# State-space heads: y products of all eight heads of a group in one burst, gating moved to later weight chunks

## The reference, cut to what matters

```
cum    = cumsum(dt * a)                                # per head, over the tokens
decay  = exp(where(causal, cum_i - cum_j, -inf))       # per head: token i, token j
cb     = C_i . B_j                                     # per group
y_i    = sum_j (cb * decay)_ij * (x_j * dt_j)          # per head, 64 columns
y      = (y + d_skip * x) * silu(z)
y      = rms_norm(y over the 512 columns of the group)
x,B,C  = silu(causal_depthwise_conv(u @ W_xBC) + bias) # width 4
```

## Time and profile before

| | |
|---|---|
| runs | 2046.87, 2047.00, 2047.02 us |
| span of the profiled execution, first to last instruction | 2045.1 us |
| own device time of the profiled execution | not listed; the median of the runs lies 1.9 us above its span |
| PE busy | 2033.3 us (99%), 10999 matrix products |
| DVE busy | 1326.1 us (65%) |
| ACT busy | 1044.2 us (51%) |
| POOL busy | 14.5 us (1%) |
| mean granted clock of PE | 0.999 |
| bytes moved by DMA | 388.12 MB, mean 190 GB/s |

### The profile page before, as it was taken

How to read it: one execution, slowest core, us unless ns; L and a number is a source line. 1 busy time by engine, 2 the same in 40 slices (tenths; PEclk the granted TensorE clock), 3 DMA queues, 4 the chain that set the end, 5 groups by cost and what they waited for, 6 DMA issues and landing times.

```text
span 2045.1 us, 31288 instructions
## 1 busy us (share of the span) xinstructions
PE 2033.3 (99%) x10999; PEld 1746.4 (85%) x10999; DVE 1326.1 (65%) x1897; ACT 1044.2 (51%) x1313; POOL 14.5 (1%) x29
## 2 busy tenths in 40 slices
PE   9999999999999999999999999999999999999998
PEld 8888888888888888998888888888888888888886
DVE  7788888888864444676555576665665665444476
ACT  6566666665554444445444465444444444444464
POOL 0000000000000000000000000000000000000000
PEclk9999999999999999999999999999999999999999
DMA  8666666666565565445556656666666666555554
GB/s 236 197 195 192 186 196 192 177 194 195 165 206 189 185 201 185 129 123 175 190 186 227 241 171 197 185 187 194 185 194 188 183 194 226 193 191 193 204 197 144
DMA packets 332351, 388.12 MB, mean 190 GB/s; under 512 B 25896, under 2 KB 248608, under 8 KB 330624
## 3 DMA queue, kind: packets, MB, share of 16 engines
q1 hardware_dynamic: 329184, 369.86, 58.0%
q0 software_dynamic: 2928, 17.21, 2.4%
q10 hardware_dynamic: 176, 0.20, 0.0%
HBM read 384.00 MB, written 3.21 MB: 189 GB/s over the span
## 4 chain that ended last, share of the span: by engine, by line
PE 99%; DMA 0%; DVE 0%; ACT 0%; SPq 0%; issue 0%; DVEq 0%
PE acc L508 16%; PE acc L521 15%; PE acc L727 14%; PE acc L728 14%; PE acc L729 14%; PE acc L526 8%; PE acc L510 8%; PE acc L666 1%; PE acc L898 1%; PE acc L484 1%; PE acc L486 1%; PE acc L485 1%; PE acc L824 1%; DMA raw<-w_in_in 0%; PE acc L589 0%; PE acc L761 0%
## 5 line engine op out<-in xcount | busy, mean ns | idle before, releaser
L1576 DVE TENSOR_TENSOR wlo<-raw,whi 128x1024 fp32r<-128x1024 f32 (+1 forms) x703 | 849.3, 1213 | 558.8 <-ACT whi L1118 556.9
L1118 ACT ACTIVATE whi<-raw 128x1024 fp32r<-128x1024 f32 (+1 forms) x704 | 736.1, 1049 | 680.1 <-PE acc L729 398.8
L508 PE MATMUL acc<-u,whi 128*128 128x512 f32 x1408 | 488.6, 394 | 0.0
L510 PE MATMUL acc<-u,wlo 128*128 128x256 f32 x1408 | 390.2, 277 | 0.0
L727 PE MATMUL acc<-whi,g 128*128 128x512 f32 x848 | 330.2, 389 | 0.0
L729 PE MATMUL acc<-whi,g 128*128 128x512 f32 x848 | 329.9, 389 | 0.0
L728 PE MATMUL acc<-wlo,g 128*128 128x512 f32 x848 | 329.9, 389 | 0.0
L521 PE MATMUL acc<-u,whi 128*128 128x512 f32 x1376 | 328.7, 391 | 0.0
L508 PEld LDWEIGHTS acc<-u,whi 128*128 128x128 f32 x1408 | 264.0, 187 | 61.4 <-issue 0.2
L521 PEld LDWEIGHTS acc<-u,whi 128*128 128x128 f32 x1376 | 252.7, 188 | 48.8
L510 PEld LDWEIGHTS acc<-u,wlo 128*128 128x128 f32 x1408 | 264.3, 188 | 0.0
(11 more groups left out here) (329 smaller groups left out, 1545.9 us busy)
## 6 DMA issues: line engine op xcount, KB each, us to landing
raw<-w_in_in SPq DMA_DIRECT2D x208, 512.0 KB, 4.1
raw<-w_gate_in SPq DMA_DIRECT2D x88, 512.0 KB, 4.5
raw<-w_up_in SPq DMA_DIRECT2D x88, 512.0 KB, 4.5
raw<-w_down_in SPq DMA_DIRECT2D x88, 512.0 KB, 3.6
raw<-w_ssm_o_in SPq DMA_DIRECT2D x64, 512.0 KB, 4.0
raw<-w_in_in SPq DMA_DIRECT2D x64, 256.0 KB, 4.1
raw<-w_attn_o_in SPq DMA_DIRECT2D x32, 512.0 KB, 4.2
raw<-w_out_in SPq DMA_DIRECT2D x32, 512.0 KB, 4.5
```

Source lines behind the costliest of these rows:

```text
L508: T.matmul(bank(b), wh[:, j, i * P:i * P + P], src[:, kt, :, :].rearrange("p a s -> p (a s)"), start=start and j == 0, stop=False, skip_gr ...
L510: last = T.matmul(bank(b)[:, 0:SEQ], wl[:, j, i * P:i * P + P], src[:, kt, 0, :], start=False, stop=stop and j == len(kts) - 1, skip_group ...
L1118: S.activation(whi[:, slot, 0:w], raw[:, slot, 0:w], ACT.Copy).then_inc(sem("hi_ready"), 1)
L1576: V.tensor_tensor(wlo[:, slot, 0:w], raw[:, slot, 0:w], whi[:, slot, 0:w].bitcast(F32), ALU.subtract) \
```

## The change: what it does

- PE: the products behind chunk 4 go away, and all four pairs of heads are multiplied behind chunk 10, in one piece. Pairs 0 and 1 go to the two halves of bank 7, pairs 2 and 3 to those of bank 6 (`y_place`). PE signals `y_mm` after two pairs, not after each.
- `e` has eight slots and a place of its own in SBUF. `decays` waits no longer for PE. Its calls for pairs 2 and 3 move from chunks 8 and 9 to 7 and 8, the Exps from 9 and 10 to 8 and 9, the masks from 9 and 10 to 8 and 9.
- DVE: `y_gate` of pairs 0 and 1 moves from chunks 8 and 9 to chunk 12, that of pairs 2 and 3 from chunks 13 and 14 to chunk 14.
- Convolution of x pair 1, `conv_first` on ACT and `conv_rest` on DVE: from chunk 11 to chunk 13.
- The SBUF area reserved for the descriptors of POOL's DMAs shrinks from 16384 to 2048 bytes of each partition, which makes room for the larger `e`.

```diff
+SCRATCH = 2048
...
-    START = 16512
-    CONST0 = START
+    START = SCRATCH + 128
+    E0 = START
+    CONST0 = E0 + HPG * 384 * 4
...
-    e = at("e", [P, 4, 384], G0 + 32 * 2048)
+    e = at("e", [P, HPG, 384], E0)
...
+    def y_place(p):
+
+        return 7 - p // 2, p % 2 * SEQ
...  PE, ssd_step
-            if c_ in (4, 10):
-                p0 = 0 if c_ == 4 else 2
-                if p0 == 0:
-                    pe.wait_ge(sem("xdt_ready"), it * 2)
-                else:
-                    pe.wait_ge(sem("y_skip"), it * 4 - 2)
-                pe.wait_ge(sem("masked"), it * 8 - 8 + 2 * p0 + 4)
-                for p in (p0, p0 + 1):
-                    b = 7 - p % 2
+            if c_ == 10:
+                pe.wait_ge(sem("xdt_ready"), it * 2)
+                pe.wait_ge(sem("masked"), it * 8)
+                for p in range(4):
+                    b, at_col = y_place(p)
...
-                    last.then_inc(sem("y_mm"), 1)
+                    if p % 2:
+                        last.then_inc(sem("y_mm"), 1)
...  ACT, ssm_main
-            if c_ in (11, 15):
-                i = (c_ - 11) // 4
+            if c_ in (13, 15):
+                i = (c_ - 13) // 2
                 if not head:
                     act.wait_ge(sem("y_skip"), it * 4 + (2 * i - 2))
                 conv_first(it, 1 + i, (2 * i, 2 * i + 1))
...  ACT, ssm_side
-            if c_ in (5, 6, 9, 10):
+            if c_ in (5, 6, 8, 9):
...  DVE, ssm_main
-            if c_ == 11:
+            if c_ == 13:
                 conv_rest(it, 1, (0, 1))
...  DVE, decays
-                if hd >= 4:
-                    dve.wait_ge(sem("y_mm"), it * 4 - 4 + (hd - 4) // 2 + 1)
...  DVE, y_gate
-            dve.wait_ge(sem("y_mm"), it * 4 - 3 + p)
+            dve.wait_ge(sem("y_mm"), it * 2 - 1 + p // 2)
...  DVE, ssm_side
+            if c_ == 7:
+                decays(it, 2)
             if c_ == 8:
+                decays(it, 3)
+                mask_scores(it, 2)
+            if c_ == 9:
+                mask_scores(it, 3)
+            if c_ == 12:
                 y_gate(it, 0)
-                decays(it, 2)
-            if c_ == 9:
-                decays(it, 3)
                 y_gate(it, 1)
-                mask_scores(it, 2)
-            if c_ == 10:
-                mask_scores(it, 3)
-            if c_ == 13:
+            if c_ == 14:
                 y_gate(it, 2)
-            if c_ == 14:
                 y_gate(it, 3)
...
-    nc = bacc.Bacc("TRN2", target_bir_lowering=False, num_devices=1)
+    nc = bacc.Bacc("TRN2", target_bir_lowering=False, num_devices=1, dynamic_dma_scratch_size=SCRATCH)
```

More of the change, by code:

```diff
@@ L652, in ssd_step @@
                 last.then_inc(sem("xtr_mm"), 1)
-            if c_ in (4, 10):
-                p0 = 0 if c_ == 4 else 2
-                if p0 == 0:
-                    pe.wait_ge(sem("xdt_ready"), it * 2)
-                else:
-                    pe.wait_ge(sem("y_skip"), it * 4 - 2)
-                pe.wait_ge(sem("masked"), it * 8 - 8 + 2 * p0 + 4)
-                for p in (p0, p0 + 1):
-                    b = 7 - p % 2
-                    ea, eb = e[:, 2 * p % 4, :], e[:, (2 * p + 1) % 4, :]
+            if c_ == 10:
[3 more added lines that the diff above has]
+                    b, at_col = y_place(p)
                     for blk, o, n in ((0, 0, 256), (1, 256, 128)):
-                        for i, ee_ in enumerate((ea, eb)):
+                        for i in range(2):
                             half = slice(64 * i, 64 * i + 64)
-                            last = T.matmul(bank(b)[half, SEQ - n:SEQ], xdt[:, blk, p, half], ee_[:, o:o + n],
-                                            start=blk == 0, stop=blk == 1, skip_group_check=True,
-                                            tile_position=(0, 64 * i))
-                    last.then_inc(sem("y_mm"), 1)
+                            last = T.matmul(bank(b)[half, at_col + SEQ - n:at_col + SEQ], xdt[:, blk, p, half],
+                                            e[:, 2 * p + i, o:o + n], start=blk == 0, stop=blk == 1,
+                                            skip_group_check=True, tile_position=(0, 64 * i))
+                    if p % 2:
+                        last.then_inc(sem("y_mm"), 1)
             if c_ == 14:
@@ L1229, in ssm_side @@
                 S.preload_act_table_set("natural_log_exp_and_others")
-            if c_ in (5, 6, 9, 10):
-                p = (5, 6, 9, 10).index(c_)
+            if c_ in (5, 6, 8, 9):
+                p = (5, 6, 8, 9).index(c_)
                 for hd in (2 * p, 2 * p + 1):
                     act.wait_ge(sem("seg"), it * 16 - 16 + 2 * hd + 2)
-                    S.activation(e[:, hd % 4, :], e[:, hd % 4, :], ACT.Exp).then_inc(sem("decay"), 1)
+                    S.activation(e[:, hd, :], e[:, hd, :], ACT.Exp).then_inc(sem("decay"), 1)
             if c_ == 14:
@@ L1755, in decays @@
             for hd in (2 * p, 2 * p + 1):
-                if hd >= 4:
-                    dve.wait_ge(sem("y_mm"), it * 4 - 4 + (hd - 4) // 2 + 1)
                 for blk, o, n in ((0, 0, 256), (1, 256, 128)):
-                    V.tensor_scalar(e[:, hd % 4, o:o + n], cumb[:, hd, SEQ - n:SEQ], cum_g[:, blk, hd:hd + 1],
+                    V.tensor_scalar(e[:, hd, o:o + n], cumb[:, hd, SEQ - n:SEQ], cum_g[:, blk, hd:hd + 1],
                                         0.0, ALU.subtract, ALU.min).then_inc(sem("seg"), 1)
@@ L1764, in mask_scores @@
                 dve.wait_ge(sem("decay"), it * 8 - 8 + hd + 1)
-                V.tensor_tensor(e[:, hd % 4, :], e[:, hd % 4, :], cbm[:, :], ALU.mult).then_inc(sem("masked"), 1)
+                V.tensor_tensor(e[:, hd, :], e[:, hd, :], cbm[:, :], ALU.mult).then_inc(sem("masked"), 1)
         def x_dt(it, blk):
@@ L1780, in y_gate @@
             V.scalar_tensor_tensor(yb[:, p % 2, :], xs[:, p, :], gp_side[:, 4 + p:5 + p],
-                                       bank(7 - p % 2)[:, 0:SEQ], ALU.mult, ALU.add).then_inc(sem("y_skip"), 1)
+                                       bank(y_place(p)[0])[:, y_place(p)[1]:y_place(p)[1] + SEQ], ALU.mult, ALU.add).then_inc(sem("y_skip"), 1)
             dve.wait_ge(sem("y_skip"), it * 4 - 3 + p)
```

## The result

Five runs of the changed kernel gave 2058.68 to 2058.95 us, median **2058.8 us**, against 2047.0 us before: ratio 1.0058, 95% interval 1.0047 to 1.0069: slower, by 0.6%. The prediction was 2058.9 us. The profiled execution has a span of 2057.2 us (12.1 more than before).

The account below looks back on a forecast made before the run. PE bounds the kernel, never waiting in the changed stretch. Per loop group 1.81 + 0.10 - 0.19 = +1.72 us, +12.0 over seven, -0.19 in the last: +11.9, giving 2058.9 us; range 2053 to 2065 us.

Parts of the forecast that it names:

- The signs to look for: Seven PE waits of 1.3 us at the squares' product, seven of 0.5 at chunk 16; loop groups of 62.4 us.
- The queue of DVE: DVE's work from the burst's start: squares ready after 15.44 us, split of chunk 16 after 18.98 us.
- B: Start of PE's burst behind chunk 10, from which the forecast counts all later times in a loop group.
- PE's need: After the burst's start PE reaches the squares' product at 14.14 us and would start chunk 16 at 17.17 us.
- The restart: PE's cost of restarting after the wait at chunk 16: 0.1 us per group, bounds 0 and 0.5.
- The passages: PE going in and out of a burst, paid once instead of twice: -0.19 us per group, -1.5 us in all.
- The last group: Group beside `cq`, no convolution queued: squares ready at 13.1 us, before 14.14, so no wait and only -0.19 us.
- Cover: Earlier masks, moved loads, POOL's `cumb` load and the next group's start make nothing late: 0 us.
- No wait: Rival: DVE's work behind the burst fits, PE never waits, only 1.5 us saved: 2045.5 us; chance 0.10.
- Spread: Rival: slower gates or convolution, or late chunk 15, carry lag to chunks 17 to 19: 2071 us; chance 0.06.
- Clock: Rival: PE's pauses drop the granted clock for one chunk per loop group, 20 us more: 2078 us; chance 0.02.
- Descriptor area: Rival: the smaller area makes POOL's transfers late, PE loses up to 4 us: 2063 us; chance 0.02.

Follow-up runs that it names:

- gates-at-12 kernel: The changed kernel with the gates of pairs 2 and 3 moved from chunk 14 to directly behind those of pairs 0 and 1 at chunk 12: 2044.4 us, 0.9988.

## Why the prediction was right, point by point

- *The signs to look for.* Seven waits at the squares' product: 1.24 us in the view, said 1.3. Seven at chunk 16: 0.21 in the view, said 0.5. From start to start, as the forecast counted, they are 15.38 - 13.98 = 1.40 and 1.86 - 1.40 = 0.46 (the terms stand below). Some 4 us of DVE before the first gate: 4.71. Loop group 62.35, said 62.4. A last group without a wait at the squares: so it was, but it got another wait, below.
- *The queue of DVE.* Forecast B + 15.44, measured B + 15.38; to chunk 16 forecast 18.98, measured 18.88. Adding single rows of before, start to next start, was exact to 0.1 us over 15 us because the queue ran without overlap: each step either stood on DVE or was ACT's answer to the step ahead of it. The gates-at-12 kernel proves the second half: with the Square beside other work the same instructions end 2.05 us earlier.
- *PE's need.* Forecast 14.14 and 17.17. With no wait it is 13.98 and, half of 3.68 us after 308.39 in the gates-at-12 rows, 17.02. The burst is 0.15 us shorter than 2 x 1.45. So chunk 16 is late by 18.88 - 17.02 = 1.86, forecast 1.81.
- *The restart.* 320.02 - 318.08 = 1.94 us for 8 high products against half of 3.65 elsewhere: 0.11, taken as 0.1.
- *The passages*, the term that was mis-sized. I took 0.19 us per group and held up to twice that possible. Measured: 8 low products take 1.04 before the burst and 1.06 behind it, where half of 1.91 is usual, so 0.19 outside, as read from the earlier trace rows. Another 0.15 is inside, since a burst of 16 takes 1.45 and one of 32 takes 2.75 us. Together 0.34, times 8 = 2.7 us and not 1.5; a group without waits is 60.38 us long, and 60.70 before. The kernel with all gates at chunk 12, which has the burst and no waits, shows it whole: 2046.9 - 2.7 = 2044.2, measured 2044.4. The Trainium skill ("TensorEngine Tiling (Array Packing)", Tiling Modes) says that a change of tiling mode drains the array, without a price. No run isolates such a change here. Part of the loss has another source: behind four full-width products of 128 columns (L657), which aren't in column halves, 8 low products take 1.03 us too (rows of the changed kernel).

```profile
276.77 1.20 PE L532 MATMUL acc<-u,wlo 128*128 128x256 f32 x8
277.80 3.82 PE L527 MATMUL acc<-u,whi 128*128 128x512 f32 x16
```

- *The last group*, a wait I had not seen: PE waits 0.4 us for `acc_q` of the `cq` phase. From start to start it costs 0.7: between PE's products over the squares and over `acc_q` lie 574.36 - 562.58 = 11.78 us, before 562.46 - 551.25 = 11.21, and the latter products then take 0.78 instead of 0.67 us. DVE's work for it stands behind the norm, and that behind the later gates. I had checked only what the squares need there, and taken the rest of the queue as free.
- *The sum.* 7 x (1.86 + 0.11) - 8 x 0.34 + 0.7 = 13.8 - 2.7 + 0.7 = +11.8 us, against 12.1 in the spans and 11.8 in the medians. The forecast was 11.9. That it agrees so closely is in part luck: a saving 1.2 us too small, a loss in the loop 0.4 too small, and 0.7 unseen in the last group nearly cancel. I also took the median to lie 1.9 us above the span; for the changed kernel it is 1.7, which makes up for the span being 0.2 above my 2057.0.
- *Cover.* The masks, the moved loads and the start of the next group cost nothing, as said. One transfer came close: ACT waits 3.43 us for `raw` ahead of its split of chunk 13, and `whi` is there at 299.29, 3.2 us before DVE takes it up (302.48). I had not listed it; the wait at the gates hides it. In the whole kernel ACT waits for these loads 18.6 us in 10 pieces, before 5.0 in 4.
- *The rivals.* No wait: shown false as the kernel stands, but it is what moving the gates or the burst reaches (2044.4, 2045.0 us). Spread: false, groups are even at 62.35. Clock: false here and behind the pauses of 1.70 us, true in five of seven groups for a pause 0.95 us longer, so the 0.02 that I gave it was for a step that lay closer than I knew. Descriptor area: false by its own run.

## What to carry to other kernels

When PE never waits, judge a move by one queue: take the event that now releases it, add every instruction that stands behind it on its engine and on the engine that answers, and compare with when PE needs the result; busy shares don't enter. Batching was worth 2.5 us here (2046.9 to 2044.4, with no wait left), and became a loss only because the last consumer was placed so late that another engine's part (the Square) had nothing to hide behind: batch the consumers as well, or move the producer up by a step. When there are two waits in a row, look at how late the last one is: removing the first gave nothing.

## What the runs showed of the hardware

- A burst of products in two column halves cost PE 0.19 us in the full-width products around it, and bursts of 16 and 32 such products took 1.45 and 2.75 us, so 0.15 us came with each burst whatever its length: 0.34 us in all. What part is owed to the change from full width to halves was not isolated.
- Behind a pause of PE of 2.19 us the granted clock fell to the 1.2 GHz level in five of seven cases, and cost about 1.1 us each beside the pause; behind pauses of 1.24 and of 1.70 us in none of seven each. Pauses between 1.70 and 2.19 us were not tried.
- Waits of PE of 0.32 and 0.25 us for a split left no entry in the view of PE's waits. PE's records overlap the next start by 0.16 us, so that the view's 0.21 us in the changed kernel was a delay of some 0.38 us (317.70, where the 8 high products from 315.87 end at their usual pace, to 318.08). The weight loads listed the short ones, as 0.26 and 0.37 us; in PE's own timeline they are seen only in runs of one product that take longer than their neighbours, and in the length of the group.
- With the descriptor area an eighth as large POOL's transfers landed no later: `wp` after 7.8 to 12.8 us (9.0 to 13.0 before), `cumb` after 4.8 to 7.7 (6.2 to 7.9).
